# Two plain gathers a token, summed by TensorE: the last stage of a hybrid MoE layer, rearranged over the engines

## What is computed

```python
act = jax.nn.silu(hg) * hu * combine[:, :, None]
ff = jnp.einsum('nef,efd->nd', act, w_down)          # sum over a token's two experts
x = layer_norm(ALPHA * x + (1 + g2) * ff, ln2_g, ln2_b)

def layer_norm(x, g, b):
    mu = jnp.mean(xf, -1, keepdims=True)
    xc = xf - mu
    var = jnp.mean(xc * xc, -1, keepdims=True)
    return xc * lax.rsqrt(var + LN_EPS) * g + b
```

## Time and profile before

| | us |
|---|---|
| median of 3 runs | 1526.51 (1523.59 to 1528.07) |
| the profiled execution | 1528.06 |
| its span in the profile | 1526.3 |
| the last stage in it | from about 1403 to 1526.3 |
| TensorE, VectorE busy over the span | 1302.6, 1269.0 |

### The profile page before, as it was taken

The page is one execution under the profiler, slowest core; times in us unless marked ns, Lnnn a source line. Parts: engine busy times, 40 slices in busy tenths (PEclk is TensorE's granted clock), DMA queues, the critical chain, the costliest instruction groups (busy, mean ns, idle before and its releaser), DMA issues. The chain is left out here.

```text
span 1526.3 us, 25848 instructions
## 1 busy us (share of the span) xinstructions
PE 1302.6 (85%) x8231; PEld 721.1 (47%) x8231; DVE 1269.0 (83%) x3124; ACT 777.7 (51%) x1327; POOL 703.2 (46%) x530
## 2 busy tenths in 40 slices
PE   5488899999999999999996537999999999996665
PEld 3345455555555555555554323444444444442221
DVE  2527799999999999999998487999999999993688
ACT  2412244334444444334444206898988888884122
POOL 0112256676776766677765422222222222211786
PEclk9789999999999999999998768999999999998798
DMA  9965431111111101111111195659993554222896
GB/s 310 300 211 178 156 122 50 56 42 56 56 56 56 56 29 42 56 43 56 42 48 42 69 330 187 248 202 331 338 383 107 191 186 149 107 109 87 211 253 199
DMA packets 106688, 219.40 MB, mean 144 GB/s; under 512 B 11796, under 2 KB 71000, under 8 KB 104547
## 3 DMA queue, kind: packets, MB, share of 16 engines
q1 hardware_dynamic: 82662, 141.23, 27.3%
q0 software_dynamic: 11808, 43.00, 10.0%
q10 hardware_dynamic: 12125, 34.01, 5.7%
HBM read 166.68 MB, written 51.56 MB: 143 GB/s over the span
## 5 line engine op out<-in xcount | busy, mean ns | idle before, releaser
L1159 DVE SCALAR_TENSOR_TENSOR y_sum<-uT,w_dw_cols,y_sum 128x128 f32<-128x128 f32 (+1 forms) x1780 | 461.7, 343 | 0.0
L2107 DVE SCALAR_TENSOR_TENSOR w_gate_up_lo<-w_gate_up_ring,w_gate_up_hi 128x2048 f16<-128x2048 f16 x96 | 219.5, 2288 | 35.8 <-ACT w_gate_up_hi L2029 35.3
L2029 ACT ACTIVATE w_gate_up_hi<-w_gate_up_ring 128x2048 f16 x96 | 182.8, 1906 | 53.9 <-issue 52.8
L1401 PE MATMUL bank<-w_in_hi,hT_hi 128*128 128x512 f16 (+3 forms) x544 | 194.3, 357 | 10.6 <-ACT late L998 9.6
L2010 POOL COPY slot_index<-slot_token 128x1 int32 (+1 forms) x48 | 57.9, 1205 | 309.9 <-PE eturn L2171 305.5
L1401 PE MATMUL bank<-w_in_lo,hT_hi 128*128 128x512 f16 (+3 forms) x544 | 194.2, 357 | 0.0
L1401 PE MATMUL bank<-w_in_hi,hT_lo 128*128 128x512 f16 (+3 forms) x544 | 194.0, 357 | 0.0
L2150 PE MATMUL ps_up<-w_gate_up_hi,slot_rowsT_hi 128*128 128x512 f16 x384 | 147.2, 383 | 26.2 <-DVE slot_rowsT_lo L2132 26.0
L2150 PE MATMUL ps_up<-w_gate_up_lo,slot_rowsT_hi 128*128 128x512 f16 x384 | 146.8, 382 | 0.0
L2150 PE MATMUL ps_up<-w_gate_up_hi,slot_rowsT_lo 128*128 128x512 f16 x384 | 146.6, 382 | 0.0
L2138 DVE SCALAR_TENSOR_TENSOR w_down_lo<-w_down_ring,w_down_hi 128x2048 f16<-128x2048 f16 x48 | 109.6, 2284 | 4.1 <-ACT w_down_hi L2083 3.8
(11 more groups left out here) (302 smaller groups left out, 2873.2 us busy)
## 6 DMA issues: line engine op xcount, KB each, us to landing
expert_rows<-out_rows ACTq DMA_DIRECT2D x48, 512.0 KB, 3.1
late<-in_w_ada SPq DMA_DIRECT2D x22, 1024.0 KB, 7.3
w_gate_up_ring<-in_w_gate SPq DMA_DIRECT2D x16, 1024.0 KB, 8.7
w_gate_up_ring<-in_w_up SPq DMA_DIRECT2D x16, 1024.0 KB, 11.6
w_down_ring<-in_w_down SPq DMA_DIRECT2D x16, 1024.0 KB, 12.3
x_h<-in_x_prompt SPq DMA_DIRECT2D x16, 512.0 KB
x_res<-in_x_prompt SPq DMA_DIRECT2D x16, 512.0 KB, 3.5
hidden<-late SPq DMA_DIRECT2D x16, 512.0 KB, 2.6
```

The lines of the kernel that those rows point to most:

```text
L1159: dve.scalar_tensor_tensor(total, u, w, y_sum[:, c, :n], ALU.mult, ALU.add).then_inc(taps_done, 1)
L1401: mm = pe.matmul(out, x[xp][:, k, :n], w[wp][:, k, cols], start=(k == 0 and wp == xp), stop=(k == KD - 1 and xp == 1))
L2029: act.activation(gate_up_parts[0][:, at, k:k + KD // 2, :, :].rearrange("p k a n -> p (k a n)"), w_gate_up[:, bass.ds(b, 1), k:k + KD // 2 ...
L2107: dve.scalar_tensor_tensor(flat[1], w_gate_up[:, bass.ds(b, 1), k, :, :].rearrange("p b k a n -> p (b k a n)"), W_SCALE, flat[0], ALU.mult ...
```

## The change

Only `finish` is edited.

- GpSimd's two gathers of a tile are both plain copies into two buffers of `picked`, which is now a ring of five tiles with two rows a token. One semaphore counts both. The right half's offset on GpSimd is gone; the power stays.
- TensorE adds the two rows: for each half, two products of the identity with the gathered rows, into a new PSUM tile `ps_s` (two of them). `sums(t)` is issued ahead of `residual(t - 1)`.
- VectorE's gate reads the sum from `ps_s` and writes `gated_rows`. Statistics, aggregation, shift, gain and half offset are replaced by an addition of epsilon on one column (`variance`), and two operations over 1024 columns (`norm`): (y + negative mean) times gain, then times root plus offset.
- ScalarE copies `ps_v` (now two of 1024 columns) to `y` with the sum of each row on the side, scales that sum to the negative mean, and squares `y` minus mean with the sum of squares on the side. At the start it scales the gain row once by the root of 1024, since the squares are summed, not averaged.
- `y` is a ring of five tiles.

```diff
-PICK_RING, Y_RING, SUM_RING = 7, 3, 4
+PICK_RING, Y_RING = 5, 5
...
-        picked = sb("expert_pick", [P, PICK_RING, D])
+        picked = sb("expert_pick", [P, PICK_RING, 2, D])
+        gated_rows = sb("gated_rows", [P, 2, D])
...
-                        pool.indirect_dma_start(out=picked[:, b, :], out_offset=None, in_=expert_rows[:, :],
-                                                in_offset=offset, compute_op=ALU.add).then_inc(both_picked[b], 16)
...
+                    if t >= PICK_RING:
+                        pool.wait_ge(summed, 2 * (t - PICK_RING) + 2)
+                    for s in range(2):
+                        pool.indirect_dma_start(out=picked[:, b, s, :], out_offset=None, in_=expert_rows[:, :],
+                                                in_offset=bass.IndirectOffsetOnAxis(ap=K["pair_slot"][:, t, s:s + 1], axis=0)).then_inc(both_picked[b], 16)
...
+                act.activation(rows[:, 2, :], rows[:, 2, :], ACT.Copy, scale=D ** 0.5).then_inc(gain_scaled, 1)
...
+                    act.activation(y[:n, yb, :], ps_v[t % 2][:n, :], ACT.Copy, accum_out=small[:n, b, 0:1]).then_inc(copied, 1)
+                    act.wait_ge(copied, t + 1)
+                    act.activation(small[:n, b, 1:2], small[:n, b, 0:1], ACT.Copy, scale=-1.0 / D).then_inc(mean_ready, 1)
+                    act.wait_ge(mean_ready, t + 1)
+                    if t >= 1:
+                        act.wait_ge(squared, t)
+                    act.activation(square[:n, :], y[:n, yb, :], ACT.Square, bias=small[:n, b, 1:2], accum_out=small[:n, b, 2:3]).then_inc(squared, 1)
...
+                        dve.tensor_tensor(gated_rows[:n, t % 2, cols], ps_s[t % 2][:n, cols], rows[:n, 0 if t == 0 else 1, cols], ALU.mult).then_inc(gated, 1)
...
+                    dve.tensor_scalar(small[:n, b, 3:4], small[:n, b, 2:3], D * EPS_SCALED, None, ALU.add).then_inc(eps_added, 1)
...
+                    dve.scalar_tensor_tensor(y[:n, yb, :], y[:n, yb, :], small[:n, b, 1:2], rows[:n, 2, :], ALU.add, ALU.mult).then_inc(gained, 1)
+                    dve.wait_ge(rstd_ready, t + 1)
+                    dve.wait_ge(gained, t + 1)
+                    dve.scalar_tensor_tensor(y[:n, yb, :], y[:n, yb, :], small[:n, b, 4:5], rows[:n, 3, :], ALU.mult, ALU.add).then_inc(offset_added, 1)
...
+                for t in range(TILES + 2):
+                    if t < TILES:
+                        gate(t)
+                    if t >= 2:
+                        variance(t - 2)
+                        norm(t - 2)
...
+                            mm = pe.matmul(ps_s[t % 2][:n, cols], ident[:n, :n], picked[:n, b, s, cols], start=(s == 0), stop=(s == 1))
+                        mm.then_inc(summed, 1)
...
+                for t in range(TILES + 1):
+                    if t < TILES:
+                        sums(t)
                     if t >= 1:
+                        residual(t - 1)
```

More of the change, by code:

```diff
@@ L2277, in power @@
[L2277 to L2287, removed]
@@ L2307, in _ @@
-                offset(TILES - 1)
+                    if t >= PICK_RING:
[3 more added lines that the diff above has]
+                                                in_offset=bass.IndirectOffsetOnAxis(ap=K["pair_slot"][:, t, s:s + 1], axis=0)).then_inc(both_picked[b], 16)
+                for t in range(PICK_RING - 1):
+                    pick(t)
@@ L2311, in _ @@
                 for t in range(TILES):
[L2312 to L2313 removed]
+                    b, n, yb = t % 4, rows_in(t), t % Y_RING
+                    act.wait_ge(added, 2 * t + 2)
                     if t >= Y_RING:
                         act.wait_ge(y_stored[yb], 16 * (t // Y_RING))
[L2316 to L2318 removed]
+                    if t >= 4:
+                        act.wait_ge(offset_added, t - 3)
@@ L2344, in shift @@
[L2344 to L2353, removed]
-                    dve.tensor_tensor(y[:n, yb, 0:512], y[:n, yb, 0:512], rows[:n, 3, 0:512], ALU.add).then_inc(offset_added, 1)
@@ new lines, in _, with sums, residual @@
+            @block.tensor
+            def _(pe):
+                def sums(t):
+                    b, n = t % PICK_RING, rows_in(t)
+                    pe.wait_ge(both_picked[b], 32 * (t // PICK_RING + 1))
+                    for h in range(2):
+                        cols = slice(h * 512, (h + 1) * 512)
+                        if t >= 2:
+                            pe.wait_ge(gated, 2 * (t - 2) + h + 1)
+                        for s in range(2):
+                            mm = pe.matmul(ps_s[t % 2][:n, cols], ident[:n, :n], picked[:n, b, s, cols], start=(s == 0), stop=(s == 1))
+                        mm.then_inc(summed, 1)
+                def residual(t):
+                    n = rows_in(t)
+                    g, x1 = x1_tile(F, W, t)
+                    pe.wait_ge(F["x1_loaded"][g], 16 * len(X1_GROUPS[g]))
+                    for h in range(2):
+                        cols = slice(h * 512, (h + 1) * 512)
+                        if t >= 2:
+                            pe.wait_ge(copied, t - 1)
+                        pe.matmul(ps_v[t % 2][:n, cols], ident[:n, :n], x1[:n, cols], start=True, stop=False)
+                        pe.wait_ge(gated, 2 * t + h + 1)
+                        pe.matmul(ps_v[t % 2][:n, cols], ident[:n, :n], gated_rows[:n, t % 2, cols], start=False, stop=True).then_inc(added, 1)
```

99 lines of the change are left out of this document (28 added, 71 removed).

## The result

The changed kernel takes 1540.37 us at the median (1538.1 to 1542.42); the kernel before, run beside it, 1525.05 (1522.24 to 1528.07). The ratio of the new time to the old is 1.0106, with a 95% interval from 1.0087 to 1.0124: about 1.1% slower. The forecast was 1543, slower, with 1536 to 1553 as its range. The profiled execution of the changed kernel took 1538.1 us, its span is 1536.2.

A forecast was written before the change was run, and what follows sets the result against it. The prediction took VectorE to bound the kernel before, at 5.53 us a tile, and TensorE after, at 6.88. Start 1409.6 + work 117.0 + clock 5.9 + drain 0.2 + tail 9.9 = 1542.6 us of span; forecast 1543, range 1536 to 1553.

The forecast's parts named there:

- start: Last stage: second gather waits for nothing, so TensorE's first sum begins at 1409.6 us, after a gather issued at 1403.90.
- work: TensorE in the last stage: 17 x 8 = 136 products at 0.86 us, 117.0 us at the full clock.
- clock: TensorE's first products of the stage: 11.8 us at half speed lose 5.9 us; ends nothing lost and 9.5.
- drain: TensorE's last product: it lasts 1.02 us against 0.86 to the next start, adding 0.2 us.
- tail: After TensorE's last product: ScalarE, addition, two wide operations, power and store, 9.9 us, give or take 1.
- the +5 that stood as upper end: Start of the stage: a late second gather, at the longest landing of 9.3 us, adds 5 us.
- Rival 1: TensorE: passes overlap more in a dense stream, a product takes less than 0.86 us, time about 1500 us; chance 0.05.
- rival 2: TensorE's clock doesn't stay at the full level: four more spells give 1550 us, a quarter at half speed 1572; chance 0.06.
- What was named as cover: Other engines in the last stage: VectorE 4.5 us, GpSimd about 3.5, DMA at most 6.1 a tile, all below TensorE's 6.88.
- GpSimd's 3.5 us a tile: GpSimd in the last stage: two gather issues at 0.95 us plus the power, about 3.5 of 6.88 us a tile.
- The stage now runs at VectorE's pace: Last stage of the kernel before: VectorE works 22.7 of 25 us and sets 5.53 us a tile, TensorE runner-up.

## Why the prediction was right, term by term

The sum of spans was: start, work, clock, drain, tail. By the stage, counted from the first gather's issue:

- **Start.** Forecast 5.7 us from the issue to TensorE's first sum; measured 6.7 (1397.07 to 1403.78). The second gather no longer waits for the first, as said, but with ten issued in a row it landed after 5.43 us, not the 4.34 of the first one in the earlier trace rows. So TensorE started 1.0 us later than forecast, inside the +5 that stood as upper end.
- **Work.** 136 products at 0.86 us, 117.0 us. Right, and the pivotal term. Four of TensorE's last products, a pair of passes each, as in the earlier trace rows:

```profile
1523.75 1.02 PE L2354 MATMUL ps_v<-w_gate_up_ring,ident 128*128 128x512 f32 x2
1524.61 1.02 PE L2356 MATMUL ps_v<-gated_rows,ident 128*128 128x512 f32 x2
1525.46 1.02 PE L2354 MATMUL ps_v<-w_gate_up_ring,ident 128*128 128x512 f32 x2
1526.32 1.02 PE L2356 MATMUL ps_v<-gated_rows,ident 128*128 128x512 f32 x2
```

They stand 0.86 apart after 100 us without a pause. Rival 1 (passes overlap more in a dense stream) is out, by this and by the version with one row.
- **Clock.** Forecast 5.9 us lost, measured about 6.5 (13.36 for eight products that take 6.9). The pattern was a little different from the one forecast: the lower level lasted through tile 0's and nearly all of tile 1's sums, but tile 0's residual, also 64 rows, passed at the full level from 1417 on, since two tiles' sums stand ahead of it. Afterwards the clock stayed at 1.00 (1420 to 1525 us), and rival 2 is out.
- **Drain and TensorE's whole.** From 1403.78 to 1526.32 + 1.02 = 1527.34: 123.6 us, against 117.0 + 5.9 + 0.2 = 123.1.
- **Tail.** Forecast 9.9, measured 1536.2 - 1527.34 = 8.9. The second wide operation ends at 1531.82 + 1.28 = 1533.10, and from there to the end, the store, were 3.1 us, not the 3.7 that I had taken from GpSimd's last operation in the earlier trace rows; ScalarE's part and the hand-overs make up the other 0.4. ScalarE's copy, for which the prediction took 1.01 us without showing how it came from the rows, took 1.02. The wait for the power beside a wide operation, which no row of before had, I had put at 0.5; it was 0.44. The last tile's timeline:

```profile
1528.76 1.15 ACT L2298 ACTIVATE f_square<-y_rows,f_small 128x1024 f32<-128x1024 f32 x1
...
1529.82 0.18 ACT L2298 ACTIVATION_READ_ACCUMULATOR f_square<-y_rows,f_small 128x1 f32 x1
1530.04 0.15 DVE L2317 TENSOR_SCALAR f_small<-f_small 128x1 f32<-128x1 f32 x1 [0.36 <-ACT f_square L2298]
1530.11 1.28 DVE L2321 SCALAR_TENSOR_TENSOR y_rows<-y_rows,f_small,final_rows 128x1024 f32<-128x1024 f32 x1
1530.27 1.52 POOL L2279 TENSOR_TENSOR f_small<-f_small,mhalf 128x1 f32<-128x1 f32 x1 [1.91 <-DVE f_small L2317]
1531.82 1.28 DVE L2324 SCALAR_TENSOR_TENSOR y_rows<-y_rows,f_small,final_rows 128x1024 f32<-128x1024 f32 x1 [0.44 <-POOL f_small L2279]
```

The errors, +1.0, +0.6 and -1.0 with 0.1 less elsewhere, almost cancel; the stage came out 0.4 us from the forecast. That the terms cancel so well is luck, while the pivotal one, the work, was right by itself.

The median rests on one thing more. The forecast is 16.3 us on top of 1526.51, the median of three executions; with a fourth that median is 1525.05, and the changed kernel's lies 15.3 us above it. The spans of the two profiled executions differ by only 9.9 us, because the stages that both share ended 6.8 us earlier in the trace of the changed kernel. No term of the sum stands for that, so the difference of these two spans is no test of the forecast; the stage and the medians are.

- **What was named as cover.** VectorE 4.5 us of work and waiting in 6.88, GpSimd and ScalarE free, the DMA engines below TensorE's pace: all stay below TensorE in the stretch from 1475 to 1500 (VectorE 13.7 of 25, ScalarE 10.2, GpSimd 16.3, DMA share 0.66), and the added work on VectorE shows the room by experiment. GpSimd's 3.5 us a tile was too low: 16.3 of 25 is 4.5 of 6.87, since one of the two issues takes 2.0 us and the power 1.5. It cost nothing here.
- **What was read too simply.** "The stage now runs at VectorE's pace" was only half of what bounded the kernel before. With VectorE relieved and no sums added, some 3 us are gained, not the 17 x (5.53 - 4.5) = 17.5 that VectorE's own relief would allow, since the gathers are next, held by the DMA engines, by GpSimd's issues or by both. It changed nothing in the sum, where TensorE was above both, but whoever had planned a better version on that sentence would have been misled.

## What to carry to other kernels

Moving a sum onto an engine that seems to have room must be priced by that engine's whole work in a tile, at the distance of its starts, against the pace of the stage: of 5.5 us 3.4 were taken and 2.1 free, and the sums asked for 3.4 more. When two engines can do the same work and each alone is too slow, divide it between them, and look first at whether the buffers and the order of issue let both run full: with the same division, two more slots and an earlier issue were worth 23 us. Wide products whose results nobody reads, ahead of a stage that begins with TensorE at its lower clock level, gave back 4 to 6 us here, together with the first sums over 128 rows (4.1, 5.9 and 6.3 in three pairs, of which the first is not clear of the noise).

## What the runs showed of the hardware

- **The lower clock lasted longer where tile 0's products had 64 rows.** With tile 0's sums over 64 rows, nearly all of the 16 passes of two tiles' sums ran at 1.2 GHz: 13.36 us, and 13.06 and 13.25 in the versions with the sums alone and with more work on VectorE. Over 128 rows the clock rose within them (9.03 us, in one trace). In the version with half by DMA and more buffers, where tile 0's 64-row residual follows at once, the granted clock was still 0.50 from 1410 to 1420 us. Once TensorE was at 2.4 GHz, 64-row products from 1417 us on kept it, at 0.86 us each.
- **An accumulating gather costs the DMA engines about twice a plain one.** The gathers' queue, over the last stage of the kernel before (1400 to 1527 us) and of the changed one (1397 to 1537 us): packets, MB, share of 16 engines' time.

```profile
q0 software_dynamic: 4896, 17.83, 62.7%
```

```profile
q0 software_dynamic: 4896, 17.83, 38.3%
```

The bytes are the same. 0.383 x 140 / 34 = 1.58 us for a plain gather; (0.627 x 127 - 17 x 1.58) / 17 = 3.1 us for an accumulating one. This is an estimate, with the plain gathers priced alike in both kernels. The other versions with accumulating gathers give 2.7 to 3.0 by the same working.
- **GpSimd's power lasts until a wide operation on VectorE has ended.** It took 0.55 us alone and 1.52 to 1.55 in all 17 tiles here; in the last it began 0.16 us after the first wide operation and ended 0.40 after its end. In the change without the sums one began 0.40 us before such an end and took 0.82. The Trainium skill, SBUF — State Buffer, section Who interferes with whom, says that a VectorE instruction with two inputs in SBUF contends with a GpSimd instruction that reads SBUF. The rows agree: 1.52 is the rest of the wide operation, 1.12, and 0.40 of its own.
